# Attention with the value products turned and taken two heads at a time, and 11 weight pieces moved from GpSimd's part of the attention into the feed-forward

## What is computed

```
h = rms_norm(x)
[qa|ka|va|qb|kb|vb] = h @ w_in
# mixer A, per head:   p = softmax(q k^T * scale + rel_bias, banded);  out = p @ v
# mixer B, per head:   p = softmax(q k^T * scale with a sink, windowed); out = p @ v
x = x + concat(A, B) @ w_out
gate, up = split(rms_norm(x) @ w_gate_up)
y = silu(causal_conv(gate)) * up
x = x + y @ w_down
```

## Time and profile before

| | |
|---|---|
| time, median of 3 runs | 2562.65 us (2561.45 to 2565.75) |
| span of the profiled execution, first to last instruction | 2559.8 us |
| TensorE busy | 2427.8 us, 95% |
| attention, first score product to last copy of the output | 496.3 to 948.3 us |
| one full tile of the attention | 27.9 us |
| VectorE / ScalarE / GpSimd busy in a full tile | 19.5 / 20.0 / 23.0 us |

### The profile page before, as it was taken

One profiled execution on the slowest core, in us unless ns is written; L12 is line 12 of the kernel. 1 busy time (PEld: TensorE's weight loads), 2 busy tenths in 40 slices (PEclk: granted clock), 3 DMA queues, 4 the chain that ended last, 5 costly groups with the idle time before them and its releaser, 6 DMA issues. The chain is left out here.

```text
span 2559.8 us, 46391 instructions
## 1 busy us (share of the span) xinstructions
PE 2427.8 (95%) x15365; PEld 2316.4 (90%) x15365; DVE 1727.1 (67%) x3780; ACT 1164.5 (45%) x2658; POOL 992.7 (39%) x1150
## 2 busy tenths in 40 slices
PE   6999999589999989998999999999999999999997
PEld 4888888489999979998899999989999998999997
DVE  7656665466766756767676666767666787676765
ACT  6232322377777653335434444543444454444433
POOL 2888888557878868831220000213000021000001
PEclk9999999789999999999999999999999999999999
DMA  8676776655666759889687666868766677666765
GB/s 260 211 222 208 219 220 194 165 142 156 187 172 166 187 155 347 293 317 336 216 294 220 215 209 221 298 233 310 224 214 216 217 268 271 213 214 214 221 207 179
DMA packets 318205, 577.88 MB, mean 226 GB/s; under 512 B 35490, under 2 KB 167826, under 8 KB 317890
## 3 DMA queue, kind: packets, MB, share of 16 engines
q1 hardware_dynamic: 274576, 424.24, 52.7%
q0 software_dynamic: 39872, 149.75, 18.3%
q10 hardware_dynamic: 3570, 1.52, 0.3%
HBM read 444.88 MB, written 132.10 MB: 225 GB/s over the span
## 5 line engine op out<-in xcount | busy, mean ns | idle before, releaser
L2195 PE MATMUL ffn_x<-carry_big 128*128 128x352 f32 x2508 | 458.5, 324 | 11.4 <-PEq L62 5.7
L2195 PEld LDWEIGHTS ffn_x<-carry_big 128*128 128x128 f32 x2508 | 411.1, 189 | 16.8 <-issue 13.1
L2195 PE MATMUL ffn_z<-ffn_h_hi_S,carry_big 128*128 128x352 f32 x1056 | 278.4, 326 | 20.1 <-DVE carry_big L2340 13.7
L316 PE MATMUL project_z<-project_w_hi,project_h_hi 128*128 128x512 f32 (+3 forms) x680 | 255.6, 376 | 20.5 <-DVE project_w_lo L489 16.3
L316 PE MATMUL project_z<-project_w_hi,project_h_lo 128*128 128x512 f32 (+3 forms) x680 | 252.0, 371 | 0.0
L316 PE MATMUL project_z<-project_w_lo,project_h_hi 128*128 128x512 f32 (+3 forms) x680 | 251.8, 370 | 0.0
L2094 POOL TENSOR_TENSOR carry_x<-carry_x,carry_work 128x352 f32<-128x352 f32 x48 | 52.1, 1086 | 503.9 <-DVE carry_work L2458 445.4
L2088 POOL DMA_DIRECT2D carry_work<-h_sums_scratch x8 | 4.4, 552 | 577.2 <-DVE ffn_y_lo_S L2362 572.8
L2340 DVE TENSOR_TENSOR carry_big<-carry_w_raw,carry_big 128x512 fp32r<-128x512 f32 (+2 forms) x413 | 224.1, 550 | 0.6 <-ACT carry_big L2276 0.4
L949 PE MATMUL attend_o<-attend_v,attend_prob_t 128*128 (+1 forms) x1680 | 213.6, 271 | 0.0
L949 PEld LDWEIGHTS attend_o<-attend_v,attend_prob_t 128*128 128x128 f32 x1680 | 211.6, 194 | 0.6
(11 more groups left out here) (264 smaller groups left out, 6498.9 us busy)
## 6 DMA issues: line engine op xcount, KB each, us to landing
carry_big<-t_gu_scratch SPq DMA_DIRECT2D x264, 512.0 KB, 4.1
carry_big<-t_dn_scratch SPq DMA_DIRECT2D x240, 256.0 KB, 3.3
carry_w_raw<-w_gu SPq DMA_DIRECT2D x198, 256.0 KB, 4.2
t_gu_scratch<-project_quads POOLq DMA_DIRECT2D x68, 512.0 KB, 4.5
carry_w_raw<-w_dn SPq DMA_DIRECT2D x180, 128.0 KB, 3.5
project_quads<-w_quads POOLq DMA_DIRECT2D x68, 256.0 KB, 4.2
carry_w_raw<-w_o SPq DMA_DIRECT2D x24, 512.0 KB, 5.9
t_dn_scratch<-attend_quads POOLq DMA_DIRECT2D x22, 512.0 KB, 4.4
```

The lines of the kernel that those rows point to most:

```text
L316: last = nc.tensor.matmul(z[c][0:w, 0:width], h[:, k, 0:w], ww[:, k, first:first + width], start=(k == 0 and h is hi and ww is w_hi), stop ...
L2195: mm = nc.tensor.matmul(bank[:, 0:SUB], weights(c)[:, wp, k, :], (hi, lo)[a][name][:, 1 if short else k, :], start=first and k == 0 and (w ...
```

## The change

In the attention:

- `values` works on pairs. The weights are now the 64 columns of `v` of one head, and the transposed probabilities (128 queries) are moved past them. The head with i = 0 goes to PSUM partitions 0 to 63 and so to the left 64 columns of the array, the other one to 64 to 127 and the right half; the two alternate, key tile by key tile. The result is features x queries. There are 8 products a tile (4 pairs of A, at every second step; 4 of B, one a step) in place of 12, with the same number of matmuls: 840, two instructions each.
- The division needs the reciprocals along the other axis. VectorE spreads them over 64 columns per head (`rden_wide`, L1079), TensorE turns that (one 128x128 transpose per product, L944), VectorE copies it to SBUF (`copy_r`, L1095) and multiplies (`divide`, L1102), which writes the output tile `o_t` itself. `output`, `copy_o` and the tile `o` are gone.
- `t_ps` has two buffers and `prob_t` four. The product has one PSUM bank: the next product waits for the `divide` of the one before (`o_ok`).
- All loops are written out; the cached keys and values lie in tiles 14 and 15 of `keys` and `v`, in place of two tiles of their own.

In the weight pieces:

- `PREPARED` is 68, 31, 22 and 11. The 11 run in `ffn`, block 0, behind gu groups 7 to 17, in two buffers cut from `work`. `sums(1)` moves from behind group 6 to behind group 18. SyncE waits for the stores before it loads the first down sums that need them (part 4).

```diff
-PREPARED = ((0, 68), (68, 110), (110, 132))
+PREPARED = ((0, 68), (68, 99), (99, 121), (121, 132))
...
             def transposes(n, u):
                 k = UNITS * n + u
                 pe.wait_ge(exp_ok, k + 1)
-                if not isinstance(n, int) or k:
-                    pe.wait_ge(t_act, k)
+                if k > 1:
+                    pe.wait_ge(t_act, k - 1)
...
-            def values(n, u):
-                k = UNITS * n + u
+            def values(n, r):
+
+                k, c = last_unit(n, r), PRODUCTS * n + r
                 pe.wait_ge(t_act, k + 1)
...
-                        last = nc.tensor.matmul(
-                            o_ps[u % 2][:, head * HEAD:(head + 1) * HEAD], prob_t[u % 2][:, src:src + P],
-                            v[:, ds(tile + j, 1), first + head * HEAD:first + (head + 1) * HEAD].rearrange("p a f -> p (a f)"),
-                            start=(j == 0), stop=(j == w - 1))
-                last.then_inc(pv_ok, 1)
...
+                for j in range(w):
+                    for i in range(2):
+                        src = prob_t[(k - 1 + i) % 4][:, j * P:(j + 1) * P] if r < PAIRS_A else \
+                            prob_t[k % 4][:, (i * w + j) * P:(i * w + j + 1) * P]
+                        first = (2 * r + i) * HEAD if r < PAIRS_A else PAIRS_A * P + i * HEAD
+                        nc.tensor.matmul(o_ps[i * HEAD:(i + 1) * HEAD, :], v[:, tile + j, first:first + HEAD], src,
+                                         start=(j == 0), stop=(j == w - 1))
+                pe.wait_ge(wide_ok, c + 1)
+                nc.tensor.transpose(r_ps, rden_wide[c % 2][:].rearrange("p a f -> p (a f)"), ident_sb[:]).then_inc(pv_ok, 1)
...
+            def copy_r(n, r):
+                c = PRODUCTS * n + r
+                dve.wait_ge(pv_ok, c + 1)
+                if c:
+                    dve.wait_ge(o_ok, c)
+                nc.vector.tensor_copy(r_sb[:], r_ps).then_inc(r_ok, 1)
...
+                nc.vector.tensor_tensor(o_t[mixer][:, r % PAIRS_A, :], o_ps, r_sb[:], ALU.mult).then_inc(o_ok, 1)
...
+                if it["b"] == 0 and not gu and it["p"] == late_part and it["i"] == 0 and q == 6:
+                    prep.stored(sp)
...
-                    if b < LAST and n == HK + 2:
+                    if b == 0 and HK + 2 < n < SUMS_AT:
+                        if n == HK + 3:
+                            prep.begin()
+                        at_n = n - HK - 3
+                        for piece in range(prep.first + prep.count * at_n // (SUMS_AT - HK - 3), prep.first + prep.count * (at_n + 1) // (SUMS_AT - HK - 3)):
+                            prep.piece(piece)
+                    if b == 0 and n == SUMS_AT:
+                        prep.stored(pool)
+                    if b < LAST and n == (HK + 2 if b else SUMS_AT):
                         sums(b + 1)
```

359 lines of the change are left out of this document (155 added, 204 removed).

## The result

The changed kernel takes 2619.7 us (median of 4 runs, 2613.45 to 2622.73) against 2562.05 us (4 runs, 2561.09 to 2565.75): ratio 1.0224, 95% interval 1.0206 to 1.0241. The prediction said 2531 us, with a range of 2502 to 2560, so it was wrong in sign and outside its range.

What follows compares the result with a forecast made beforehand. TensorE was taken to bound the attention, busy 27.70 of 27.94 us per full tile. Full tiles -30, tiles 0 to 4 -5, moved pieces +4 gave -31 us off 2562.65: about 2531 us, range 2502 to 2560.

Steps and rivals of the forecast that it cites:

- Product instructions, 0.054 us with overlap: Attention products on TensorE: both column halves run at once, 0.054 us per instruction, against 0.107 without overlap.
- Shape change, 0.3 us per group: TensorE, each of 8 product groups per tile: switching between 128x128 and 128x64 and back costs 0.3 us, 2.4 a tile.
- Group A: Product of a pair of mixer A on TensorE, with shape change and reciprocals' transpose: 1.59 us against 2.12 before.
- group B: Product of mixer B on TensorE, with shape change and reciprocals' transpose: 0.95 us against 0.83 before.
- VectorE: 24 new operations at 0.25 us: Full attention tile: spreading, copy and multiply, 8 each, add 6.0 us; VectorE goes from 19.5 to 22.0 of 25.4 us.
- I count waits of TensorE in full tiles as unchanged.: Full attention tiles: TensorE's waits stay as before, so a tile shortens by 2.5 us to 25.4 us.
- GpSimd is not the bound: Full attention tile before: GpSimd busy 22.97 of 27.94 us, so taking weight pieces out of the attention wins nothing.
- Tiles 0 to 4, -5 us: First attention tiles: output transposes go, B's products add, second `t_ps` saves 4 us; together -5 us, between 0 and -12.
- Moved pieces, +4 us (0 to 10): Feed-forward block 0: the 11 pieces' DMA traffic costs 4 us, about 9.3 us a piece, with no costly SyncE wait.
- VectorE takes over: Rival, full tiles: slack per pair is insufficient, a step pays 0.15 us more, a tile loses 1.8 us; 2553 us, chance 0.13.
- No overlap: Rival, attention products: the two column halves don't run at the same time; 2598 us, slower, chance 0.17.
- the sum per pair (0.4 us of slack): VectorE per pair of steps in full tiles: 3.7 us of work against TensorE's 4.1 us, leaving 0.4 us of slack.

Runs made afterwards that it cites:

- e10: e1 with no weight piece between GpSimd's key and query subtractions for the next tile, the attention's 31 pieces spread over the other two places: 2542.6 us, ratio 0.9918.
- e8: e10 with only the order of a pair's products changed, all of the first head and then all of the second instead of taking turns: 2569.2 us.
- e2: The changed kernel with the spreading kept in count and place, but with one of two sources in PSUM (last 2 of 136 keep the old form): 2557.9 us.
- e1: The changed kernel without the spreading operation; reciprocals go to TensorE as two 64-column weights repeating one column, multiplied with the identity: 2550.1 us.
- e6: The kernel before with only the 11 weight pieces moved from the attention into the feed-forward: 2569.4 us, ratio 1.0031.
- e4: The changed kernel with GpSimd's large key and query subtractions cut into four pieces each, spreading as it is: 2582.0 us.
- e7: The changed kernel with the attention's 31 weight pieces done in the first stage: 2777.8 us (1 run), attention 496.6 us against 509.6.
- e13: The kernel before plus an unneeded 128-column SBUF-to-SBUF spreading into a spare tile, 136 in all: 2651.8 us, ratio 1.0354.

## Why the prediction was wrong, step by step

- **Product instructions, 0.054 us with overlap.** Right, and so is the 0.107 us for one half (0.109 in e10's records). In the changed kernel 20 products start at 700.94 and the transpose of the reciprocals at 702.18: 1.24 us where 1.18 was worked out without the shape change. e8 bears out the overlap.
- **Shape change, 0.3 us per group.** Too high. Group A took 1.24 + 0.16 = 1.40 us for 1.59, group B 0.76 (717.81 over 718.40 to 718.57) for 0.95. That is 0.1 us at the far side. The near side is another 0.1 (last score product to first product 0.21 us, 700.73 to 700.94, for 0.12 before, 682.29 to 682.41), so both together are 0.2 us. That the busy time came out at 25.36 us all the same is partly luck: the products and what goes with them take 4.2 us less in e10's full tile than before (9.07 for 13.25 us, start to start), not 2.5, while scores and transposes take 2.4 us more, half of it on the near side of the shape change and in waits.
- **VectorE: 24 new operations at 0.25 us.** This is the step that failed, above all. I priced all three by the copy of 128x128 in the earlier trace rows, but that one reads PSUM. Copy and division do too, and took 0.28 us. The spreading reads and writes SBUF, took 0.948 us in the mean and up to 3.5, and put 55 us onto the attention (e2). Without the hold the sum holds: e10's VectorE is busy 19.30 us a tile, and 8 x 0.23 would make it 21.1. The attention missed its forecast by 82 us (+47 for -35): 55 are the hold, 3.5 the operation itself (e2 to e1), 10.3 the order of GpSimd's work (e1 to e10), and the last 13 are tiles of 26.12 us for 25.4 (9 us) and the short tiles.
- **"I count waits of TensorE in full tiles as unchanged."** Also wrong, by 0.6 us a tile in the best version (26.12 us with 25.50 busy), and by up to 2.8 where a piece stood ahead of the queries. "GpSimd is not the bound" was true of its sum and false of its order.
- **Tiles 0 to 4, -5 us.** Too much, within its bounds: from the first score to GpSimd's subtraction of the keys in the first full tile e1 takes 125.4 us (496.0 to 621.4), the kernel before 127.2 (496.3 to 623.5), which is -2.
- **Moved pieces, +4 us (0 to 10).** Mechanism incomplete, size within its range: e6 gives 8. I had only looked at the DMA traffic, and VectorE's operations on SBUF beside the pieces lengthen as well. A piece took 11.2 us for my 9.3 (eleven from 1314.5 to 1437.5 us in the changed kernel), but no wait of SyncE names them, as forecast.
- **The rivals.** "VectorE takes over" had the right symptoms (ScalarE waits for the maxima, TensorE for ScalarE), but with 22 us of work a slack too small by 0.15 us; that e2, with the hold removed, takes about its 2553 us (2557.9) is chance, since e2's loss is in the order of GpSimd's work. No rival had an operation that stands for another engine. "No overlap" was priced at 2598; no run took the overlap away whole, and the part that e8 took away cost 26.6 us.

**The trace of before had the row.** In the first stage VectorE has a scalar operation from SBUF to SBUF too, on 10 columns. VectorE, then GpSimd, of the kernel before:

```profile
350.56 0.17 DVE L546 SCALAR_TENSOR_TENSOR project_rq<-project_rq,project_n_y 128x10 f32<-128x10 f32 x1
350.76 1.15 DVE L548 TENSOR_SCALAR project_rq<-project_rq,project_x_r 128x10 f32<-128x10 f32 x1
```

```profile
350.58 1.31 POOL L138 TENSOR_TENSOR project_quads<-project_quads 128x512 fp32r<-128x512 f32 x1
```

Ten columns in 1.15 us, and the end at 351.91 is GpSimd's (351.89). Over its 34 uses:

```profile
L548 DVE TENSOR_SCALAR project_rq<-project_rq,project_x_r x34: 224/469/1334, 47.0 to 466.8; 128x10 f32<-128x10 f32 x16, 128x16 f32<-128x16 f32 x16, 64x10 f32<-64x10 f32 x1, 64x16 f32<-64x16 f32 x1
```

A spread from 224 to 1334 ns for one form was the sign. Had I priced the spreading by this row as the upper end, the sum per pair (0.4 us of slack) would have turned over at 0.65 us.

## What to carry to other kernels

Price a new VectorE operation by a row with its operands in the same memories, not by one of the same size, and look at the minimum and maximum beside the mean: where they are far apart, lay the other engine's timeline beside it. If VectorE must work on SBUF alone while GpSimd works, give it a source in PSUM, hand the job to another engine, or do without; here each of these two tries was worth over 60 us for an operation of 0.23 us. When a stage gets shorter, check again what each engine does in which order, as its sum may still fit when its order no longer does.

## What the runs showed of the hardware

- VectorE's operation from SBUF waited for GpSimd: 50 of the 52 long spreadings ended 0.07 to 0.18 us behind the end of a GpSimd operation, 45 of them behind a subtraction of 2.4 to 2.9 us. The hold can span several GpSimd instructions (3.14 us over four of about 0.7, e4).
- The holds did not go by GpSimd's share of busy time: three subtractions, 7.7 us in a 30 us tile, gave a mean of 0.836 us (e7), and 17.8 us of work gave 0.948.
- Two 64-column halves of the array ran side by side at 0.0575 us per float32 instruction (20 in 1.15 us, e10), with 0.109 us between the starts of one half. An instruction for the free half started ahead of up to three queued for the busy one (e8).
- TensorE took weights that repeat one column without a written copy (e1): 0.31 us for four instructions, against 0.17 for one transpose and a 0.23 us operation on VectorE.
- Where TensorE waited more, its clock was at 1.2 GHz more often: one operation added on VectorE took the attention's granted clock from 0.96 to 0.91 and the busy time of the same 3625 matmuls from 433.0 to 468.6 us (e13).
